# A decode step with mLSTM and sparse attention: the causal bound by identity products, and four small moves of work

## The reference, cut to what matters

```python
z = x @ w_in + b_in                          # mLSTM and NSA columns
mix_m = sigmoid(m_o) * head_norm(mlstm_chunkwise(q, k, v, ig, lf))
mix_n = gates * (compressed, selected and window attention)
x1 = layer_norm(ALPHA * x + concat(mix_m, mix_n) @ w_out)
u = causal_dwconv(x1 @ w_up + b_up)
ff = (gelu(u[:, :D_FF]) * u[:, D_FF:]) @ w_down + b_down
y = layer_norm(ALPHA * x1 + ff)
```

```python
dmat = where(causal, b[t] - b[s] + ih[s], -inf)
w_intra = exp(dmat - m_t)                    # zero for keys after the query
a = w_intra * (q @ k)                        # then num = a @ v, and so on
```

## Time and profile before

| | |
|---|---|
| runs | 883.38, 882.62 and 879.86 us, median 882.62 |
| profiled execution, its own time | 885.9 us |
| its span in the trace | 884.0 us |
| mean granted clock of TensorE | 0.971 |
| PE busy | 830.4 us, 94% (7804 products) |
| DVE busy | 570.2 us, 64% |
| ACT busy | 424.6 us, 48% |
| POOL busy | 137.2 us, 16% |

### The profile page before, as it was taken

One profiled execution on the slowest core, in us unless ns is written; L12 is line 12 of the kernel. 1 busy time (PEld: TensorE's weight loads), 2 busy tenths in 40 slices (PEclk: granted clock), 3 DMA queues, 4 the chain that ended last, 5 costly groups with the idle time before them and its releaser, 6 DMA issues.

```text
span 884.0 us, 20066 instructions
## 1 busy us (share of the span) xinstructions
PE 830.4 (94%) x7804; PEld 757.3 (86%) x7804; DVE 570.2 (64%) x1172; ACT 424.6 (48%) x868; POOL 137.2 (16%) x257
## 2 busy tenths in 40 slices
PE   5999999798999898779999999999999999999993
PEld 5998888686888666547799999999999999999993
DVE  4633346622343789786596678888888888564645
ACT  5333245464543446757534655556555554222215
POOL 2012222433256100010000111111111110000000
PEclk9999999899999889889999999999999999999996
DMA  9267779978755000000432543222222222222312
GB/s 323 92 192 247 233 253 304 277 226 254 230 144 193 22 2 9 1 1 1 151 135 72 189 147 117 96 73 96 87 82 96 75 87 85 84 84 86 94 49 101
DMA packets 55009, 112.47 MB, mean 127 GB/s; under 512 B 7209, under 2 KB 32586, under 8 KB 54402
## 3 DMA queue, kind: packets, MB, share of 16 engines
q1 hardware_dynamic: 47074, 90.54, 31.3%
q0 software_dynamic: 6528, 17.83, 6.4%
q10 hardware_dynamic: 1312, 2.81, 1.2%
HBM read 105.54 MB, written 12.40 MB: 133 GB/s over the span
## 4 chain that ended last, share of the span: by engine, by line
PE 80%; DVE 7%; DMA 5%; ACT 3%; issue 3%; SPq 1%; POOLq 1%; POOL 0%; ACTq 0%; DVEq 0%
PE q L2012 32%; PE q L2010 30%; DMA arena<-in_pool 4%; PE q L2074 2%; PE q L2398 2%; PE q L2414 1%; PE q L2062 1%; DVE xt L1627 1%; PE q L2501 1%; PE q L2424 1%; PE q L2128 1%; DVE xt L1639 1%; PE q L2085 1%; PE q L2364 1%; PE q L2488 1%
## 5 line engine op out<-in xcount | busy, mean ns | idle before, releaser
L2010 PE MATMUL q<-arena_r,whi_r 128*128 128x256 f32 x672 | 199.2, 296 | 9.2 <-DVE wring_r L510 8.9
L2012 PE MATMUL q<-arena_r,whi_r 128*128 128x288 f32 (+1 forms) x672 | 200.2, 298 | 0.0
L2012 PE MATMUL q<-arena_r,wring_r 128*128 128x288 f32 (+1 forms) x672 | 199.8, 297 | 0.0
L507 ACT ACTIVATE whi_r<-wring 128x1024 fp32r<-128x1024 f32 (+1 forms) x99 | 102.3, 1033 | 202.9 <-PE q L2012 202.3
L2010 PE MATMUL q<-arena_r,wring_r 128*128 128x256 f32 x672 | 189.6, 282 | 0.0
L510 DVE TENSOR_TENSOR wring_r<-wring,whi_r 128x1024 fp32r<-128x1024 f32 (+1 forms) x99 | 117.8, 1189 | 100.9 <-ACT whi_r L507 100.3
L2012 PE MATMUL q<-xt_r,whi_r 128*128 128x290 f32 (+1 forms) x552 | 164.8, 298 | 0.0
L2010 PE MATMUL q<-xt_r,whi_r 128*128 128x256 f32 x552 | 155.8, 282 | 0.0
L2010 PEld LDWEIGHTS q<-arena_r,whi_r 128*128 128x128 f32 x672 | 127.8, 190 | 18.3 <-DVE wring_r L510 8.9
L2010 PEld LDWEIGHTS q<-arena_r,wring_r 128*128 128x128 f32 x672 | 127.9, 190 | 0.0
L2012 PEld LDWEIGHTS q<-arena_r,whi_r 128*128 128x128 f32 x672 | 127.8, 190 | 0.0
(11 more groups left out here) (485 smaller groups left out, 1588.5 us busy)
## 6 DMA issues: line engine op xcount, KB each, us to landing
wring<-in_w_up SPq DMA_DIRECT2D x42, 512.0 KB, 3.3
wring<-in_w_in SPq DMA_DIRECT2D x27, 512.0 KB, 5.0
arena<-in_pool SPq DMA_DIRECT2D x64, 192.0 KB, 3.9
arena<-in_pool POOLq DMA_DIRECT2D x64, 192.0 KB, 4.3
wring<-in_w_down SPq DMA_DIRECT2D x24, 448.0 KB, 3.3
wring<-in_w_out SPq DMA_DIRECT2D x8, 512.0 KB, 5.8
out_win_s<-in_win SPq DMA_DIRECT2D x8, 508.0 KB
arena<-in_pool SPq DMA_DIRECT2D x48, 64.0 KB, 2.5
```

The costliest lines, as they stand in the source:

```text
L507: return eng.activation(out, src, ACT.Copy)
L2010: pe.matmul(out[:, 0, 0:HALF], w, x[:, 0:HALF], start=(kk == 0 and n == 0), stop=(end and n == 2))
L2012: mm = pe.matmul(out[:, 1, 0:width - HALF], w, x[:, HALF:width], start=(kk == 0 and n == 0), stop=(end and n == 2))
```

## The change

It has four parts, named by letters here and in the prediction.

- **A.** VectorE begins with a memset of 128 x 512 to 1, and TensorE, once that is done, makes 18 unused products of 512 columns into bank 7 ahead of the first tile.
- **B.** GpSimd copies the identity and `causal` to fp32r tiles. In each chunk `exponents` first makes two products, identity by `causal`, of 512 columns, and the 40-row products are added to them in PSUM. `decay` goes. ScalarE's exponential reads PSUM, stands at the head of its step m = 4c+2, and writes `wx`; from the second chunk on it also waits for the `values` of the chunk before (`ml_v`), which read `wx`. `states` waits for this exponential (`ml_w`) in place of the minimum.
- **C.** The two unused products at m = 1 go. The output products of steps 27 and 28 move from the start of the step to its end, and wait for three head rows; the wait for the fourth stands after the loop.
- **D.** ScalarE's two copies into `rstd` go; VectorE waits for the spread and multiplies by its PSUM banks. TensorE makes 12 unused products of 512 columns into bank 2 ahead of the last spread.

```diff
+            pool.tensor_copy(ident_r, ident)
+            pool.tensor_copy(causal_r, causal)
             pool.memset(scp, 0.0).then_inc(prep, 1)
...
-                if 2 < m < 4 * QT + 2 and m % 4 == 3:
-                    act.wait_ge(ml_x, (m - 3) // 4 + 1)
-                    act.activation(wx, wx, ACT.Exp).then_inc(ml_w, 1)
+                if m < 4 * QT and m % 4 == 2:
+                    act.wait_ge(ml_d, m // 4 + 1)
+                    if m > 2:
+                        act.wait_ge(ml_v, m // 4)
+                    act.activation(wx, q4[1].rearrange("p b c -> p (b c)"), ACT.Exp).then_inc(ml_w, 1)
...
-            act.wait_ge(ln_pe, pe_stat(1, "spread"))
-            act.activation(rstd[:, 0:T], bank[6], ACT.Copy)
-            act.activation(rstd[:, T:NT], bank[7][:, 0:NS], ACT.Copy).then_inc(ln_act, 1)
...
+            link(dve.memset(mixt_r[:, KD - 1, 0:512].bitcast(F32), 1.0))
...
-            def decay(c):
-                dve.wait_ge(ml_d, c + 1)
-                dve.tensor_tensor(by_block(wx), by_block(q4[1].rearrange("p b c -> p (b c)")),
-                                  causal.unsqueeze(1).broadcast_to([128, H, 128]), ALU.min).then_inc(ml_x, 1)
...
-            mlstm = (decay, carry, products, divided)
+            mlstm = (carry, products, divided)
...
-            dve.wait_ge(ln_act, 8)
+            dve.wait_ge(ln_pe, pe_stat(1, "spread"))
+            deviation = q4[3].rearrange("p b c -> p (b c)")[:, 0:NT]
             for m in range(KD):
-                dve.tensor_tensor(xt[:, m, :], xt[:, m, :], rstd, ALU.mult).then_inc(ln_u, 1)
+                dve.tensor_tensor(xt[:, m, :], xt[:, m, :], deviation, ALU.mult).then_inc(ln_u, 1)
...
+            pe.wait_ge(dve_step, 1)
+            for _ in range(18):
+                pe.matmul(bank[7], mixt_r[:, KD - 1, 0:128], mixt_r[:, KD - 1, 0:512], start=True, stop=True)
...
                 else:
+                    pe.wait_ge(prep, 4)
                     pe.wait_ge(tok_v_ev, QT + 1)
                     pe.wait_ge(tok_k_ev, 2 * QT + 2)
                 for q in range(2):
+                    pe.matmul(by_block(bank[2 + q]), ident_r, causal_r.unsqueeze(1).broadcast_to([128, 4, 128]),
+                              start=True, stop=False, skip_group_check=True)
+                for q in range(2):
                     p = slice(64 * q, 64 * q + 40)
-                    mm = pe.matmul(bank[2 + q], gl[p, token_rows(c)], rows[p, c % 2, :], start=True, stop=True)
+                    mm = pe.matmul(bank[2 + q], gl[p, token_rows(c)], rows[p, c % 2, :], start=False, stop=True,
+                                   skip_group_check=True)
...
-                pe.wait_ge(ml_x, c + 1)
+                pe.wait_ge(ml_w, c + 1)
...
-                if m == 27:
-                    pe.wait_ge(ml_mx, 4)
-                    pe.wait_ge(m_lo, 1)
-                    pe.wait_ge(w_lo, I_OUT + 1)
-                if m in (27, 28):
-                    out_products(0, (2 * m - 54, 2 * m - 53), 0)
...
-                    unused_products(4, 2)
...
+                if m == 27:
+                    pe.wait_ge(ml_mx, 3)
+                    pe.wait_ge(m_lo, 1)
+                    pe.wait_ge(w_lo, I_OUT + 1)
+                if m in (27, 28):
+                    out_products(0, (2 * m - 54, 2 * m - 53), 0)
...
             pe.wait_ge(m_lo, 7)
+            pe.wait_ge(ml_mx, 4)
...
+            for _ in range(12):
+                pe.matmul(bank[2], mixt_r[:, 0, 0:128], mixt_r[:, 1, 0:512], start=True, stop=True)
             spread(1)
```

More of the change, by code:

```diff
@@ L340, in layer @@
         kcp = work[:, 4312:4344].rearrange("p (g c) -> p g c", g=NG)
+        ident_r, causal_r = raw_lo[:, KD - 1, 104:232], raw_lo[:, KD - 1, 232:360]
         mxs = work[:, 3856:3872].rearrange("p (n g) -> p n g", g=NG)
@@ L1735, in _ @@
                     cmp_probs(i)
-                if 2 <= m < 4 * QT + 2:
-                    mlstm[(m - 2) % 4]((m - 2) // 4)
+                if 3 <= m < 4 * QT + 2 and m % 4 != 2:
+                    mlstm[(m - 3) % 4]((m - 3) // 4)
                 if 6 <= m < 4 * QT + 6 and m % 4 == 2:
@@ L2347, in _ @@
             b7, b6 = bank[7], bank[6]
-            def unused_products(b, n):
-                for _ in range(n):
-                    pe.matmul(bank[b], xt_r[:, KD - 1, 104:232], xt_r[:, KD - 1, 232:488].unsqueeze(1).broadcast_to([128, 2, 256]), start=True, stop=True)
             COLUMNS = ((3, range(Z_MK, Z_MK + 4)), (6, (Z_CK, Z_CV, Z_SV, Z_WV)), (2, range(Z_MV, Z_MV + 4)))
```

## The result

| | before | after |
|---|---|---|
| median of 20 runs | 885.14 us | 878.98 us |
| lowest and highest | 879.37, 890.04 | 871.60, 888.71 |
| profiled execution, its own time | 885.9 us | 876.34 us |
| its span | 884.0 us | 874.4 us |

The ratio after to before is 0.9931 (95% interval 0.9908 to 0.9953). That is 6.1 us of 885.1, where the sum of the prediction had 12.1. The change made the kernel faster, by half of what was forecast. The ratios leave out runs more than 1.5% above the fastest of the same kernel, so they need not be the quotient of the medians.

The account below looks back on a forecast made before the run. TensorE bounds the projections and loop's end, VectorE the pair loop's middle, with half-clock stretches besides. Terms -1.9 - 7.5 - 0.5 - 2.2 = -12.1 from 885.9 gave 873.8 us, adjusted to 872.2; range 866 to 879.

Parts of the forecast that it names:

- -1.9 forecast: Start of the kernel: unused products before the first tile save 1.9 us; ends +0.8 and -1.9.
- the first step: Part A: the first tile starts at 8.94 us and runs at the fast pace, its inputs arriving in time.
- As TensorE has no gap from 22 to 100, the shift stays: Projections: the 1.9 us gained at the start is kept, since TensorE is busy throughout 22 to 100 us.
- -7.5 forecast: Decays in the pair loop's four chunks: -4.1 us of work and -3.4 us of clock.
- The clock comes on top: Chunks 0 and 1: shorter TensorE rests remove much of two half-clock stretches, -1.5 and -1.9 us; ends 0 and -5.3.
- The first rival: The clock falls after chunks 0 and 1 all the same; -8.7 us remains, about 875.6; chance 0.20.
- The work term: Four chunks without VectorE's minimum: -0.6 in chunk 0, -1.3 in chunk 1, -1.1 each in 2 and 3; together -4.1 us.
- the fourth rival: Pair loop: ScalarE's exponential makes copies late, +4.2 us, and two more clock falls, +6.8; ends at 889; chance 0.04.
- -0.5 forecast: Pair loop's end: moved output products save 0.5 us, half clock expected to stay; ends +1 and -3.
- -2.2 forecast: Kernel's end: ScalarE's copies go (nearly all of 1.2 us), the spread runs at full clock; ends -2.4 and +1.0.
- The reference point: Start value for the sum: middle between profiled 885.9 us and shown median 882.62, moving 873.8 to 872.2.
- rivals 1 and 3: 1: clock falls after chunks 0 and 1 anyway, 875.6, chance 0.20; 3: loop gives nothing, 878, chance 0.07.

Follow-up runs that it names:

- only_d: The kernel before with part D alone; median 884.21 us, ratio 0.9984.
- after_no_b: The kernel after without part B, the two unused products at m = 1 kept; median 884.78 us, ratio 1.0001.
- fill_no_ident: fill_after without the identity products, so the causal bound is left out; median 870.49 us, ratio 0.9825.
- The two filled kernels: Before and after, each with unused products put into its own rests; medians 879.05 us (ratio 0.9952) and 872.60 us (0.9876).
- fill_after: The kernel after with unused products of 256 columns ahead of eight waits of TensorE; median 872.60 us, ratio 0.9876.
- its four edits: fill_after without part B 875.75 us, without identity products 870.49, without part A 873.80, with the output stage's 14 unused products moved to another wait 868.58.

## Why the prediction was wrong in B, and right in A, C and D

**A: -1.9 forecast, -2.1 at the start.** All of the first step holds: the mean of the first tile is 8.30 us in the six traces without A and 6.15 in the eight with it. That the number of slow products differs from run to run, as the prediction quoted, shows in the six (17 to 26). "As TensorE has no gap from 22 to 100, the shift stays" looked at no more than that stretch: behind it, from 100 to 262, TensorE waits for pages some 10 us in every execution. Whether the lead is partly lost there was not settled.

**B: -7.5 forecast, -2.6 measured at full clock, and nothing clear of noise from the clock.** This is the step that failed, in both its terms. "The clock comes on top" (-3.4) took the two stretches at half clock for a consequence of two rests that the change shortens. Two of the three traces with B and unfilled rests have 17.1 us at half clock there, more than the 13.7 of before. The rest of 1.13 us ahead of the value products of chunk 0, which B leaves almost as it was (1.18 in only_d), stands ahead of both. In the runs, B alone has 51.9 us at half clock for 52, and after 44.3 for the 50.8 of after_no_b: the first is nothing, the second 2.5 us of time at 0.39 with a standard error of 1.4. The first rival, in which the clock falls all the same, was what happened.

The work term (-4.1) was mis-sized: chunks 0 and 1 gave 1.1 for 1.9, chunks 2 and 3 1.45 for 2.2. The minima's waits did go (4.9 us of rest). But each pair of identity products takes 0.65 to 0.69 us, where the prediction had 0.43 in chunks 0 and 1 and next to nothing in chunks 2 and 3; leaving them out gave 1.1 us in all (fill_no_ident). And the waits for VectorE's `products`, the next of the same chain, grew by 0.8 us. Without the identity products it would have been 3.7. In chunks 2 and 3 the sum let TensorE follow VectorE, since VectorE was full; with B TensorE is busy 32.32 of 33.69 us there, 1.3 us more than without it, and its two added products a chunk are paid for. That ScalarE's exponential from PSUM costs no more was right: 1.024 us against 1.055, and the fourth rival, late copies, did not come: TensorE waits 3.4 us for copies in the loop, as before (3.5).

**C: -0.5 forecast, -0.6 at full clock.** Right. That the half clock round pair 27 would stay was right as well: it lasted 6.8 us in four traces without the move, 3.4 in three with it and 10.2 in a fourth, all with unfilled rests.

**D: -2.2 forecast, -1.9.** Right but for the term that was not looked up: VectorE's centred rows end at 872.80 in the trace of before, so its wait of 1.95 us was the most that could be had. The 12 products took 3.05 us for the 2.6 of the prediction and were still done in time, but they do not always hold the clock.

**The reference point.** The middle between the profiled execution and the median shown (882.62, of three runs) took the latter for a typical value. Over 20 runs the median of before is 885.14. The measured 878.98 lies just inside the upper end of the range (879), which was set by rivals 1 and 3 and not by the forecast.

The parts at full clock, with A whole, make 2.1 + 2.6 + 0.6 + 1.9 = 7.2 us; with A lost 5.1. The measured 6.1 lies between (4.9 by the means). The two filled kernels, both at full clock in most of the loop, differ by 6.8 us in the mean (standard error 1.3).

## What to carry to other kernels

Where TensorE's clock falls after rests, read each stretch at half clock as a draw of that execution, and size an edit by stretches at the same clock in both traces; a few unused products put into the rests make such stretches, and here they were worth more than the edit. When a wait is taken away in a chain that goes to and fro between engines, look at the next wait of the same chain (one that half clock hides in a trace is still there at full clock), and add to the sum what the full engine has to do more.

## What the runs showed of the hardware

- Five rests of 1.05 to 2.76 us in an otherwise busy TensorE were followed by 3.4 to 6.8 us at half clock in after, two of 1.14 and 1.24 us were not; filled with unused products of 256 columns, none of those in the pair loop was, neither in fill_after nor in its four edits. Why the same rest is followed by half clock in one execution and not in another was not tried. The Trainium skill (TensorE: Matmul & The Clock Gate, "HAM oscillation") tells of waits for DMA that send the clock down in every tile; here waits for VectorE and ScalarE inside a loop do it, and not in every execution.
- VectorE's product with an operand in PSUM took 0.716 us for 128x544, from SBUF before 0.723. The 0.5 us over eight that the prediction worked out from the Trainium skill's errata (VectorE: DVE Perf Modes) as a price does not show.
- With 18 products of 512 columns ahead of it the first tile took 6.14 to 6.16 us in eight traces; without them 7.91 to 8.83 in six.
